# A hybrid encoder trunk with its token rows in another order: row p of tile t holds token 2p+t

## The chip, the cores and the metric

One core of one Trainium2 chip runs the whole kernel in one launch. The metric is the device time in microseconds (us); of several executions the median counts. Before the change it is 1027.39 us.

## What is computed

The trunk has two layers over 256 tokens of 1024 channels, all float32. Each layer does

```python
h = rms_norm(x, attn_pre_norm)
gates, mla_in, dil_in, diff_in = split(h @ w_in)
merged = g_mla * (mla(mla_in) @ w_branch_mla) + g_dil * (dilated(dil_in) @ w_branch_dil) \
       + g_diff * (diff(diff_in) @ w_branch_diff)
x = x + rms_norm(merged @ w_out, attn_post_norm)
h = rms_norm(x, ffn_pre_norm)
u = h @ w_up                                   # 1024 -> 2 x 2816
u = sum(shift(u, t - 1) * conv_w[t] for t in range(3))     # along the tokens
x = x + rms_norm((gelu(u_gate) * u_val) @ w_down, ffn_post_norm)
```

Two parts care about the order of the tokens. The convolution reads each token's two neighbours. The dilated attention has three groups: in the first a token sees the tokens at most 64 away, in the second those of its own class modulo 4, in the third those of its own class modulo 16 (at 256 tokens the radius excludes none of them). Everything else treats tokens alike, so long as queries, keys, values and outputs agree on which row is which token.

## The kernel before

The 256 tokens lie as two tiles of 128 rows (`x[128, 2, 1024]`). Row 64h+j of tile t holds token 4j+2t+h: each tile has two of the four classes modulo 4, one in each half of its rows. So for the second and third group of the dilated attention a tile needs only its own 128 keys. This order is set where x and the positions are loaded (lines 465, 704) and undone where the output is stored (`class_rows`, line 506).

Precision is kept by splitting: a value v becomes `hi` (a rounded copy) and `lo` = v - hi, and each product takes three matmuls, hi·lo, lo·hi and hi·hi (`passes`, line 1456). The weights pass through a ring of three buffers in 1 MB pieces, in the fixed order of `plan_pieces`. SyncE loads piece n once its buffer's `lo` has been written, ScalarE writes `w_hi` (`split_hi`, line 727), VectorE writes `w_lo` (`split_lo`, line 1083), and TensorE uses the piece. `STEPS`, one list written by `plan_steps`, is walked by TensorE, ScalarE and VectorE alike, and each does its own part of a step in that order; semaphores alone hold them together.

The MLP works the other way round. Its activations `hT` (channels on the rows, tokens on the columns) must be in true token order, since the convolution runs along the columns. `turn_ffn` (line 1722) turns x by transposes into PSUM; ScalarE's `ffn_hi` (line 839) and VectorE's `ffn_lo` (line 1110) write them to `hT_hi` and `hT_lo` through `tile_tokens` (line 536), which picks the columns of tile t: `[:, :, 2t:2t+2]` of groups of four, so two adjacent columns and then a gap of two. `scale_rows` (line 1125) does the same for the row of scales. These steps stand in "mid", between the attention sublayer and the MLP, where TensorE has nothing else but `keep_clock` transposes.

The MLP is planned in units u = 0..10: two pieces "up" (gate and value channels, 256 each; TensorE gets 128 channels by 256 tokens into PSUM), and two units later one piece "down". For each unit VectorE scales (lines 1134 to 1141), ScalarE and VectorE do the three taps of the convolution (lines 980, 1408, 1414), ScalarE the gelu (line 986), VectorE the product (`gated`, line 1148). Then ScalarE's `gated_hi` (line 858) and VectorE's `gated_lo` (line 1153) make `g_hi` and `g_lo`, and here they put the columns back in the order of the rows of x, by reading every fourth column:

```python
nc.scalar.activation(by_class2(g_hi[:, u % G_RING, :]), own_order2(conv[:, u % 2, 1, :]), ACT.Copy)
V.tensor_tensor(by_class2(g_lo[...]), own_order2(conv[...]), by_class2(g_hi[...]), ALU.subtract)
```

The piece "down" takes 128 adjacent columns of `g_hi` or `g_lo` as its stationary operand (`lhs_of`, line 1488) and 512 columns of the weights as the moving one: 2 k x 4 tiles x 3 passes = 24 matmuls a piece, 264 in a layer (the last piece of a layer takes its first tiles through `last_rows`, lines 1538 to 1544). TensorE waits for `g_lo_done` before a piece "down". In an even "up" step VectorE's order is: scale the piece, `split_lo` of a later one, `gated_lo` of the unit two before, then the convolution.

At the end of a layer ("end") ScalarE and VectorE split the first two pieces of the next layer, then do the squares (line 872), the gain (line 1256) and the residual (line 1268) of each tile, with the root from GpSimd (lines 637 to 642); TensorE turns the new x (line 1646) and goes on.

At the start GpSimd builds the mask (lines 592 to 612) while x is loaded. VectorE's `other_classes` (lines 1045 to 1052) turns row-minus-column distances, 128 columns, into the mask of the third group, then `rope_angles` follows, both in the step after piece 1; then comes `split_lo` of the pieces that TensorE needs next. GpSimd adds the result to the mask (line 653).

Of the kernel before, what the change touches and what calls it, by code (L numbers as in the profile page):

```python
# [16 lines left out]
P = 128  # L17
# [291 lines left out]
def build_trunk(nc, a, out):  # L309
    with ExitStack() as ctx:  # L310
# [111 lines left out]
        other_class = rope_b[:, 0:P]  # L422
# [42 lines left out]
        tokens = a["x"][0].rearrange("(j t h) d -> h j t d", t=NT, h=2)  # L465
# [34 lines left out]
        def own_order2(cols):  # L500
            return cols.rearrange("p (c j r) -> p c r j", c=2, r=4)

        def by_class2(cols):
            return cols.rearrange("p (c r j) -> p c r j", c=2, r=4)

        def class_rows(dram):

            view = dram[0].rearrange("(j r) d -> r j d", r=4)
            return [(slice(64 * (r % 2), 64 * (r % 2) + 64), r // 2, view[r]) for r in range(4)]
# [26 lines left out]
        def tile_tokens(cols, t):  # L536

            return cols.rearrange("p (j r) -> p j r", r=4)[:, :, 2 * t:2 * t + 2]
# [5 lines left out]
        def store_rows(eng, r_odd):  # L544

            for t in range(NT):
                for h in range(2):
                    s = slice(h * 512, h * 512 + 512)
                    part, t_of, dst = class_rows(out)[2 * t + r_odd]
                    eng.wait_ge(x_ready, X_START + 8 * DEPTH - 4 + 2 * t + h + 1)  # L550
                    eng.dma_start(dst[:, s], x[part, t_of, s]).then_inc(out_landed, 16)
# [29 lines left out]
        def _(pool):  # L581
# [13 lines left out]
            for t in range(NT):  # L595
                for h in range(2):
                    rq = 2 * t + h
                    m = mask[64 * h:64 * h + 64, t, 0:SEQ].rearrange("p (r j) -> p r j", r=4)
                    nc.gpsimd.affine_select(out=m, in_=m, compare_op=ALU.is_ge, fill=MASKED, base=rq + 64,
                                            pattern=[[-1, 4], [-4, 64]], channel_multiplier=4)  # L600
                    pool.drain()
                    nc.gpsimd.affine_select(out=m, in_=m, compare_op=ALU.is_ge, fill=MASKED, base=64 - rq,
                                            pattern=[[1, 4], [4, 64]], channel_multiplier=-4)
                    pool.drain()

            for t in range(NT):
                for g in range(2):
                    c0 = SEQ + P * g
                    nc.gpsimd.memset(mask[0:64, t, c0 + 64:c0 + 128], MASKED)
                    pool.drain()  # L610
                    nc.gpsimd.memset(mask[64:128, t, c0:c0 + 64], MASKED)
                    pool.drain()


# [29 lines left out]
            for l in range(DEPTH):  # L644
# [5 lines left out]
                if l == 0:  # L650
                    pool.wait_ge(class_ready, 1)
                    for t in range(NT):
                        nc.gpsimd.tensor_tensor(mask[:, t, 384:512], mask[:, t, 384:512], other_class, ALU.add)
# [46 lines left out]
        def _(act):  # L700
# [3 lines left out]
            positions = a["positions"][0, :].rearrange("(j t h) -> h j t", t=NT, h=2)  # L704
# [129 lines left out]
            def ffn_hi(l, t, pairs):  # L834

                for pair in pairs:
                    act.wait_ge(turn_full, l * NTURN + (TURN_BEFORE["ffn"] + FFN_FULL.index((t, pair)) + 1))
                    for k in (2 * pair, 2 * pair + 1):
                        last = nc.scalar.activation(tile_tokens(hT_hi[:, k, :], t), turned_bank(t, k).rearrange("p (h j) -> p j h", h=2), ACT.Copy,
# [12 lines left out]
            def gated_hi(l, u):  # L852
# [5 lines left out]
                nc.scalar.activation(by_class2(g_hi[:, u % G_RING, :]), own_order2(conv[:, u % 2, 1, :]), ACT.Copy).then_inc(g_hi_done, 1)  # L858
# [140 lines left out]
        def _(dve):  # L999
# [45 lines left out]
            def other_classes():  # L1045

                dve.wait_ge(distance_ready, 1)
                V.tensor_scalar(distance, distance, 3, None, ALU.bitwise_and)
                dve.drain()
                V.tensor_copy(other_class, distance)  # L1050
# [55 lines left out]
            def ffn_lo(l, t, pair):  # L1106

                dve.wait_ge(turn_hi, l * NTURN + (TURN_BEFORE["ffn"] + FFN_HI.index((t, pair)) + 1))
                for k in (2 * pair, 2 * pair + 1):
                    last = V.scalar_tensor_tensor(out=tile_tokens(hT_lo[:, k, :], t), in0=turned_bank(t, k).rearrange("p (h j) -> p j h", h=2),  # L1110
# [10 lines left out]
            def scale_rows(l):  # L1121

                dve.wait_ge(scales_full, l + 1)
                for t in range(NT):
                    V.tensor_copy(tile_tokens(token_scale, t), bank[3][:, t * P:(t + 1) * P].rearrange("p (h j) -> p j h", h=2))
# [790 lines left out]
```

## Time and profile before

| what | value |
|---|---|
| median of 3 runs | 1027.39 us (1027.29 to 1027.89) |
| the profiled execution | 1026.48 us, of which the span is 1024.7 us |
| TensorE busy | 1010.8 us |
| VectorE busy | 717.8 us |
| ScalarE busy | 589.3 us |
| GpSimd busy | 132.0 us |
| granted TensorE clock, mean | 0.998 of full speed |
| moved by DMA | 170.74 MB, 167 GB/s |

The span runs from the first to the last instruction; the time adds what lies around it, 1.8 us here. In the rows below, PE is TensorE's matmul, PEld its weight load, DVE VectorE, ACT ScalarE, POOL GpSimd. PE's durations are modelled and overlap: it is the distance from one start to the next that counts, not the sum.

### The profile page before, as it was taken

What the parts mean: (1) busy time and instruction counts of PE and PEld (TensorE: products, weight loads), DVE (VectorE), ACT (ScalarE), POOL (GpSimd) and SP (SyncE); (2) the same over time, 40 slices, a digit from 0 to 9 for tenths busy, and PEclk for the clock granted to TensorE, in tenths of its full rate; (3) what the DMA queues carried; (4) which work ended last, traced back from release to release, by engine and by line L of the source; (5) the groups of instructions that cost most, each with busy time, mean ns of one, the idle gap of its engine ahead of it and who ended that gap; (6) DMA issues with size and microseconds to landing.
All of it is one profiled execution on the core that took longest, in us unless ns stands there. A gap on an engine that the chain in (4) does not pass through costs nothing.

```text
span 1024.7 us, 15035 instructions
## 1 busy us (share of the span) xinstructions
PE 1010.8 (99%) x5764; PEld 883.3 (86%) x5764; DVE 717.8 (70%) x962; ACT 589.3 (58%) x859; POOL 132.0 (13%) x257
## 2 busy tenths in 40 slices
PE   8999999999999999999999999999999999999997
PEld 8889999888888988888888899998888889888886
DVE  5635566555586899999875355666555869899996
ACT  5657666565446555555575666665663556555553
POOL 3353124000001000000024321230000020000000
PEclk9999999999999999999999999999999999999999
DMA  8555445454445565555364544465335644655541
GB/s 254 184 169 161 123 132 178 165 165 164 144 135 174 186 226 174 196 190 180 123 200 160 169 131 123 143 217 164 124 127 181 203 145 166 213 198 186 184 164 42
DMA packets 109035, 170.74 MB, mean 167 GB/s; under 512 B 3377, under 2 KB 72804, under 8 KB 108964
## 3 DMA queue, kind: packets, MB, share of 16 engines
q1 hardware_dynamic: 107676, 166.88, 50.1%
q10 hardware_dynamic: 1208, 2.63, 0.8%
q8 instruction: 46, 0.75, 0.3%
q0 software_dynamic: 80, 0.26, 0.1%
q14 instruction: 25, 0.20, 0.1%
HBM read 168.72 MB, written 1.05 MB: 166 GB/s over the span
## 4 chain that ended last, share of the span: by engine, by line
PE 94%; DVE 2%; ACT 1%; DVEq 1%; issue 1%; POOL 0%; POOLq 0%; ACTq 0%
PE bank L1458 20%; PE bank L1460 19%; PE bank L1459 19%; PE high_banks L1468 10%; PE high_banks L1466 5%; PE high_banks L1864 2%; PE high_banks L1458 2%; PE high_banks L1459 2%; PE high_banks L1460 2%; PE high_banks L1465 1%; PE high_banks L1765 1%; PE high_banks L1786 1%; PE high_banks L1857 1%; PE high_banks L1774 1%; PE high_banks L1802 1%
## 5 line engine op out<-in xcount | busy, mean ns | idle before, releaser
L1083 DVE TENSOR_TENSOR w_lo<-w_raw,w_hi 128x2048 fp32r<-128x2048 f32 (+3 forms) x174 | 364.1, 2095 | 160.1 <-ACT w_hi L727 159.8
L727 ACT ACTIVATE w_hi<-w_raw 128x2048 fp32r<-128x2048 f32 (+3 forms) x174 | 305.0, 1754 | 139.0 <-PE high_banks L1468 92.5
L1458 PE MATMUL bank<-w_hi,hT 128*128 128x512 f32 (+2 forms) x700 | 258.5, 369 | 1.5 <-DVE hT L1162 0.7
L1460 PE MATMUL bank<-w_hi,hT 128*128 128x512 f32 (+2 forms) x700 | 252.9, 361 | 0.0
L1459 PE MATMUL bank<-w_lo,hT 128*128 128x512 f32 (+2 forms) x700 | 252.5, 361 | 0.0
L1468 PE MATMUL high_banks<-hT,w_hi 128*128 128x512 f32 x420 | 149.8, 396 | 0.0
L1458 PEld LDWEIGHTS bank<-w_hi,hT 128*128 128x128 f32 x700 | 131.5, 188 | 17.6 <-issue 2.9
L1460 PEld LDWEIGHTS bank<-w_hi,hT 128*128 128x128 f32 x700 | 131.4, 188 | 14.1
L1459 PEld LDWEIGHTS bank<-w_lo,hT 128*128 128x128 f32 x700 | 131.7, 188 | 13.0
L1466 PE MATMUL high_banks<-hT,w_lo 128*128 128x256 f32 x480 | 124.0, 279 | 0.0
L1466 PEld LDWEIGHTS high_banks<-hT,w_lo 128*128 128x128 f32 x480 | 90.5, 188 | 5.2
L1468 PEld LDWEIGHTS high_banks<-hT,w_hi 128*128 128x128 f32 x420 | 78.8, 188 | 16.3
L637 POOL TENSOR_SCALAR mean_squares<-small 128x1 f32<-128x1 f32 x12 | 7.6, 633 | 596.1 <-ACT x_normed L872 580.4
L980 ACT ACTIVATE conv_out<-up_scaled,par_all 128x256 f32<-128x256 f32 x88 | 40.0, 502 | 49.9 <-DVE up_scaled L1141 22.2
L1458 PE MATMUL bank<-w_hi,g_lo 128*128 128x512 f32 x168 | 66.6, 396 | 0.0
L1459 PE MATMUL bank<-w_lo,g_hi 128*128 128x512 f32 x168 | 65.5, 390 | 0.0
L1460 PE MATMUL bank<-w_hi,g_hi 128*128 128x512 f32 x168 | 65.5, 390 | 0.0
L1458 PE MATMUL high_banks<-hT,w_lo 128*128 128x256 f32 x208 | 59.2, 284 | 0.7 <-DVE hT L1110 0.7
L1459 PE MATMUL high_banks<-hT,w_hi 128*128 128x256 f32 x208 | 58.8, 283 | 0.0
L1460 PE MATMUL high_banks<-hT,w_hi 128*128 128x256 f32 x208 | 58.8, 283 | 0.0
L626 POOL TENSOR_TENSOR rope_a<-stage,cosT 128x96 f32<-128x96 f32 (+1 forms) x40 | 28.9, 723 | 164.4 <-ACT stage L746 136.2
L1139 DVE TENSOR_REDUCE up_scaled<-high_banks 128x512 f32<-128x1024 f32 x30 | 36.6, 1221 | 12.3 <-PE high_banks L1468 12.3
(244 smaller groups left out, 1508.2 us busy)
## 6 DMA issues: line engine op xcount, KB each, us to landing
w_raw<-in_w_up_dram SPq DMA_DIRECT2D x44, 1024.0 KB, 5.0
w_raw<-in_w_in_dram SPq DMA_DIRECT2D x36, 1024.0 KB, 5.0
w_raw<-in_w_in_dram SPq DMA_DIRECT2D x36, 768.0 KB, 4.3
w_raw<-in_w_down_dram SPq DMA_DIRECT2D x22, 1024.0 KB, 4.8
w_raw<-in_w_out_dram SPq DMA_DIRECT2D x8, 1024.0 KB, 5.0
w_raw<-in_w_in_dram SPq DMA_DIRECT2D x8, 672.0 KB, 4.1
w_raw<-in_w_branch_mla_dram SPq DMA_DIRECT2D x4, 1024.0 KB, 4.9
w_raw<-in_w_branch_diff_dram SPq DMA_DIRECT2D x4, 1024.0 KB, 4.9
```

The source lines that it names most:

```text
L626: nc.gpsimd.tensor_tensor(ca, xr, c, ALU.mult)
L727: nc.scalar.activation(w_hi[:, n % RING, 0:nk * cols], raw[:, n % RING, 0:nk * cols], ACT.Copy).then_inc(hi_done, 1)
L980: last = nc.scalar.activation(conv[:, u % 2, b, j * SEQ:(j + 1) * SEQ], up_scaled[:, c % 2, j, :], ACT.Copy, scale=par_all[:, l, 44 + ch:4 ...
L1083: V.tensor_tensor(w_lo[:, n % RING, s], raw[:, n % RING, s], w_hi[:, n % RING, s].bitcast(F32), ALU.subtract).then_inc(lo_done, 1)
L1139: V.tensor_reduce(up_scaled[:, c % 2, :, :], up_banks(c).rearrange("p j (s q) -> p j q s", s=2), AX.X, ALU.add).then_inc(up_summed, 1)
L1458: PE.matmul(dst, lhs[1], rhs_hi, start=start, stop=False)
L1459: PE.matmul(dst, lhs[0], rhs_lo, start=False, stop=False)
L1460: return PE.matmul(dst, lhs[0], rhs_hi, start=False, stop=stop)
L1465: PE.matmul(dst, w_parts[0], hT[:, k, :, :], start=True, stop=False)
L1466: last = PE.matmul(dst[:, 0:SEQ], w_parts[1], hT_hi[:, k, :], start=False, stop=False)
L1468: last = PE.matmul(dst, w_parts[0], hT[:, k, :, :], start=False, stop=k == KD - 1)
L1864: last = PE.transpose(T_BANK[:, b * P:(b + 1) * P], probs[:, i % 2, b * P:(b + 1) * P], ident[:])
```

## The change

The rows of x now hold token 2p+t in row p of tile t. Then a tile's tokens are every second column of the token order. The products of the MLP stay in token order, so `gated_hi` and `gated_lo` read and write adjacent columns, and the piece "down" takes every second column of `g_hi` and `g_lo` as its stationary operand. `tile_tokens` becomes every second column too, for `hT_hi`, `hT_lo` and the scales, read from adjacent columns of PSUM. A tile still holds whole classes modulo 4 (rows of one parity each), so the second and third group need their own 128 keys as before, but both masks are now made from distances, by `& 1` and `& 7`: the eight fills of half tiles go, eight half-height selections become four of full height, and VectorE's `other_classes` has one more instruction and 256 columns in place of 128 in two others. GpSimd adds 256 columns to the mask in place of 128.

```diff
-        other_class = rope_b[:, 0:P]
+        distance_8 = rope_a[:, P:2 * P].bitcast(I32)
+        distances = rope_a[:, 0:2 * P].bitcast(I32)
+        other_class = rope_b[:, 0:2 * P]
...
-        tokens = a["x"][0].rearrange("(j t h) d -> h j t d", t=NT, h=2)
+        tokens = a["x"][0].rearrange("(h j t) d -> h j t d", h=2, t=NT)
...
-        def class_rows(dram):
-            view = dram[0].rearrange("(j r) d -> r j d", r=4)
-            return [(slice(64 * (r % 2), 64 * (r % 2) + 64), r // 2, view[r]) for r in range(4)]
+        def rows_of(dram):
+            view = dram[0].rearrange("(h j t) d -> h t j d", h=2, t=NT)
+            return [(slice(64 * h, 64 * h + 64), t, view[h, t]) for t in range(NT) for h in range(2)]
...
         def tile_tokens(cols, t):
-            return cols.rearrange("p (j r) -> p j r", r=4)[:, :, 2 * t:2 * t + 2]
+            return cols.rearrange("p (m r) -> p m r", r=NT)[:, :, t]
...
             for t in range(NT):
-                for h in range(2):
-                    rq = 2 * t + h
-                    m = mask[64 * h:64 * h + 64, t, 0:SEQ].rearrange("p (r j) -> p r j", r=4)
...
-            for t in range(NT):
-                for g in range(2):
-                    c0 = SEQ + P * g
-                    nc.gpsimd.memset(mask[0:64, t, c0 + 64:c0 + 128], MASKED)
-                    nc.gpsimd.memset(mask[64:128, t, c0:c0 + 64], MASKED)
+                m = mask[:, t, 0:SEQ].rearrange("p (r j) -> p r j", r=NT)
+                nc.gpsimd.affine_select(out=m, in_=m, compare_op=ALU.is_ge, fill=MASKED, base=t + 64,
+                                        pattern=[[-1, NT], [-2, P]], channel_multiplier=2)
+                nc.gpsimd.affine_select(out=m, in_=m, compare_op=ALU.is_ge, fill=MASKED, base=64 - t,
+                                        pattern=[[1, NT], [2, P]], channel_multiplier=-2)
...
-                        nc.gpsimd.tensor_tensor(mask[:, t, 384:512], mask[:, t, 384:512], other_class, ALU.add)
+                        nc.gpsimd.tensor_tensor(mask[:, t, 256:512], mask[:, t, 256:512], other_class, ALU.add)
...
-            positions = a["positions"][0, :].rearrange("(j t h) -> h j t", t=NT, h=2)
+            positions = a["positions"][0, :].rearrange("(h j t) -> h j t", h=2, t=NT)
...
-                        last = nc.scalar.activation(tile_tokens(hT_hi[:, k, :], t), turned_bank(t, k).rearrange("p (h j) -> p j h", h=2), ACT.Copy,
+                        last = nc.scalar.activation(tile_tokens(hT_hi[:, k, :], t), turned_bank(t, k), ACT.Copy,
...
-                nc.scalar.activation(by_class2(g_hi[:, u % G_RING, :]), own_order2(conv[:, u % 2, 1, :]), ACT.Copy).then_inc(g_hi_done, 1)
+                nc.scalar.activation(g_hi[:, u % G_RING, :], conv[:, u % 2, 1, :], ACT.Copy).then_inc(g_hi_done, 1)
...
-                V.tensor_scalar(distance, distance, 3, None, ALU.bitwise_and)
+                V.tensor_scalar(distance_8, distance, 7, None, ALU.bitwise_and)
                 dve.drain()
-                V.tensor_copy(other_class, distance)
+                V.tensor_scalar(distance, distance, 1, None, ALU.bitwise_and)
+                dve.drain()
+                V.tensor_copy(other_class, distances)
...
-                    last = V.scalar_tensor_tensor(out=tile_tokens(hT_lo[:, k, :], t), in0=turned_bank(t, k).rearrange("p (h j) -> p j h", h=2),
+                    last = V.scalar_tensor_tensor(out=tile_tokens(hT_lo[:, k, :], t), in0=turned_bank(t, k),
...
-                    V.tensor_copy(tile_tokens(token_scale, t), bank[3][:, t * P:(t + 1) * P].rearrange("p (h j) -> p j h", h=2))
+                    V.tensor_copy(tile_tokens(token_scale, t), bank[3][:, t * P:(t + 1) * P])
...
-                V.tensor_tensor(by_class2(g_lo[:, u % G_RING, :]), own_order2(conv[:, u % 2, 1, :]),
-                                by_class2(g_hi[:, u % G_RING, :].bitcast(F32)), ALU.subtract).then_inc(g_lo_done, 1)
+                V.tensor_tensor(g_lo[:, u % G_RING, :], conv[:, u % 2, 1, :],
+                                g_hi[:, u % G_RING, :].bitcast(F32), ALU.subtract).then_inc(g_lo_done, 1)
...
-                return g_hi[:, u % G_RING, k * SEQ + t * P:k * SEQ + t * P + P], g_lo[:, u % G_RING, k * SEQ + t * P:k * SEQ + t * P + P]
+                own = slice(k * SEQ, (k + 1) * SEQ)
+                return tile_tokens(g_hi[:, u % G_RING, own], t), tile_tokens(g_lo[:, u % G_RING, own], t)
```

## Rows read from the trace of the kernel before

**Rows 1.** The page: busy time by engine, and the chain that ended last.

```profile
PE 1010.8 (99%) x5764; PEld 883.3 (86%) x5764; DVE 717.8 (70%) x962; ACT 589.3 (58%) x859; POOL 132.0 (13%) x257
PE 94%; DVE 2%; ACT 1%; DVEq 1%; issue 1%; POOL 0%; POOLq 0%; ACTq 0%
```

**Rows 2.** The page's costliest groups: busy us, mean ns, idle before and releaser.

```profile
L858 ACT ACTIVATE g_hi<-conv_out 128x512 fp32r<-128x512 f32 x22 | 24.9, 1133 | 9.8 <-DVE conv_out L1148 9.8
L1153 DVE TENSOR_TENSOR g_lo<-conv_out,g_hi 128x512 fp32r<-128x512 f32 x22 | 23.6, 1073 | 3.5 <-ACT g_hi L858 3.5
L1148 DVE TENSOR_TENSOR conv_out<-conv_out 128x512 f32<-128x512 f32 x22 | 15.1, 684 | 0.2
L986 ACT ACTIVATE conv_out<-conv_out 128x512 f32<-128x512 f32 x22 | 13.6, 619 | 0.0
```

**Rows 3.** Timeline (start us, us) where a "down" piece begins, the first held one.

```profile
379.81 0.40 PE L1468 MATMUL high_banks<-hT,w_hi 128*128 128x512 f32 x1
380.08 0.47 PE L1458 MATMUL bank<-w_hi,g_lo 128*128 128x512 f32 x1
380.38 0.39 PE L1459 MATMUL bank<-w_lo,g_hi 128*128 128x512 f32 x1
380.61 0.40 PE L1460 MATMUL bank<-w_hi,g_hi 128*128 128x512 f32 x1
...
380.05 0.19 PEld L1458 LDWEIGHTS bank<-w_hi,g_lo 128*128 128x128 f32 x1 [0.16 <-issue]
...
378.87 1.06 DVE L1153 TENSOR_TENSOR g_lo<-conv_out,g_hi 128x512 fp32r<-128x512 f32 x1
```

**Rows 4.** Timeline at the last held "down" piece of the second layer.

```profile
984.38 0.47 PE L1458 MATMUL bank<-w_hi,g_lo 128*128 128x512 f32 x1
```

**Rows 5.** Timeline of VectorE and TensorE at the start.

```profile
20.84 0.22 DVE L1048 TENSOR_SCALAR rope_a<-rope_a 128x128 int32<-128x128 int32 x1
21.13 0.23 DVE L1050 CAST rope_b<-rope_a 128x128 f32<-128x128 int32 x1
...
27.86 0.50 PE L1458 MATMUL bank<-w_hi,hT 128*128 128x512 f32 x1 [0.60 <-DVE w_lo L1083]
```

**Rows 6.** Timeline between the layers, then the same steps at the kernel's end.

```profile
510.89 0.60 ACT L872 ACTIVATE x_normed<-bank 128x512 f32<-128x512 f32 x1 [0.31 <-PE bank L1544]
...
509.41 3.03 DVE L1083 TENSOR_TENSOR w_lo<-w_raw,w_hi 128x1344 fp32r<-128x1344 f32 x2
513.98 1.41 DVE L1268 SCALAR_TENSOR_TENSOR x_rows<-square_ffn,roots,x_rows 128x512 f32<-128x512 f32 x2
...
1014.64 0.60 ACT L872 ACTIVATE x_normed<-bank 128x512 f32<-128x512 f32 x1 [2.76 <-PE bank L1544]
...
1017.01 1.41 DVE L1268 SCALAR_TENSOR_TENSOR x_rows<-square_ffn,roots,x_rows 128x512 f32<-128x512 f32 x2 [0.29 <-POOL roots L642]
```

**Rows 7.** Lines 839, 848, 1110, 1162: duration ns as min/median/max, first and last start.

```profile
L839 ACT ACTIVATE hT<-bank,par_all x20: 364/383/423, 324.4 to 832.4; 128x128 fp32r<-128x128 f32 x20
...
L848 ACT ACTIVATE hT<-bank,par_all x4: 360/369/382, 520.1 to 520.9; 128x128 fp32r<-128x128 f32 x4
...
L1110 DVE SCALAR_TENSOR_TENSOR hT<-bank,par_all,hT x20: 339/342/352, 326.9 to 834.7; 128x128 fp32r<-128x128 f32 x20
...
L1162 DVE SCALAR_TENSOR_TENSOR hT<-bank,par_all,hT x4: 343/345/351, 520.8 to 521.6; 128x128 fp32r<-128x128 f32 x4
```

**Rows 8.** Timeline in the first "mid" step: VectorE, and TensorE's first two pieces "up".

```profile
331.39 2.28 DVE L1083 TENSOR_TENSOR w_lo<-w_raw,w_hi 128x2048 fp32r<-128x2048 f32 x1
...
328.33 0.36 PE L1458 MATMUL high_banks<-hT,w_lo 128*128 128x256 f32 x1 [0.33 <-DVE hT L1110]
...
334.15 0.28 PE L1458 MATMUL high_banks<-hT,w_lo 128*128 128x256 f32 x1
```

**Rows 9.** Timeline of GpSimd in the second layer: rotary product for diff, then for uq.

```profile
542.49 0.46 POOL L627 TENSOR_TENSOR rope_b<-stage,sinT 128x128 f32<-128x128 f32 x1
...
554.63 0.45 POOL L627 TENSOR_TENSOR rope_b<-stage,sinT 128x128 f32<-128x128 f32 x1
```

More of the change, by code:

```diff
@@ L498, in by_class @@
             return cols.rearrange("p (r j) -> p r j", r=4)
[L500 to L504, printed above, removed]
-        def class_rows(dram):
-            view = dram[0].rearrange("(j r) d -> r j d", r=4)
-            return [(slice(64 * (r % 2), 64 * (r % 2) + 64), r // 2, view[r]) for r in range(4)]
+        def rows_of(dram):
+            view = dram[0].rearrange("(h j t) d -> h t j d", h=2, t=NT)
+            return [(slice(64 * h, 64 * h + 64), t, view[h, t]) for t in range(NT) for h in range(2)]
         def wait_tile(eng, l, m):
@@ L548, in store_rows @@
                     s = slice(h * 512, h * 512 + 512)
-                    part, t_of, dst = class_rows(out)[2 * t + r_odd]
+                    part, t_of, dst = rows_of(out)[2 * t + r_odd]
                     eng.wait_ge(x_ready, X_START + 8 * DEPTH - 4 + 2 * t + h + 1)
@@ L595, in _ @@
             for t in range(NT):
-                for h in range(2):
-                    rq = 2 * t + h
-                    m = mask[64 * h:64 * h + 64, t, 0:SEQ].rearrange("p (r j) -> p r j", r=4)
[L599 to L604, printed above, removed]
-            for t in range(NT):
-                for g in range(2):
-                    c0 = SEQ + P * g
-                    nc.gpsimd.memset(mask[0:64, t, c0 + 64:c0 + 128], MASKED)
-                    pool.drain()
-                    nc.gpsimd.memset(mask[64:128, t, c0:c0 + 64], MASKED)
-                    pool.drain()
+                m = mask[:, t, 0:SEQ].rearrange("p (r j) -> p r j", r=NT)
+                nc.gpsimd.affine_select(out=m, in_=m, compare_op=ALU.is_ge, fill=MASKED, base=t + 64,
+                                        pattern=[[-1, NT], [-2, P]], channel_multiplier=2)
+                pool.drain()
+                nc.gpsimd.affine_select(out=m, in_=m, compare_op=ALU.is_ge, fill=MASKED, base=64 - t,
+                                        pattern=[[1, NT], [2, P]], channel_multiplier=-2)
+                pool.drain()
             def rope(view, heads, first, half, t):
```

## The prediction, made before the change was run

> **What bounds the kernel now.** I read the page first: TensorE is busy for 99% of the span and 94% of the chain that ended last is matmuls [rows 1]. So a microsecond is gained only where a matmul starts late, and lost only where one starts later than now. VectorE and ScalarE have idle time on the whole. Next I went through the timeline for places where the distance between two matmul starts is above its usual one. Usual is 0.23 us after a matmul of 512 columns, as from 380.38 to 380.61 [rows 3]. The change touches four places that stand out.
>
> First, the start of a piece "down". The last matmul of the piece "up" starts at 379.81 and VectorE's g_lo ends at 378.87 + 1.06 = 379.93. Only at 380.05 does the first weight load begin, 0.16 us after TensorE could have had it, and the first matmul shows 0.47 us where others show 0.39: 0.31 us to the next start [rows 3]. From 379.81 to 380.38 it is 0.57 us where two usual distances make 0.46, so 0.11 us are lost. The wait is on g_lo, not on "issue", as the row puts it: the load starts 0.12 us after g_lo ends, every time. There are 7 such starts in each layer, 14 in all, from 380.08 to 984.38 [rows 3, 4]; the other 8 of the 22 show no 0.47.
>
> Second, the start of the kernel: at 27.86 TensorE has waited 0.60 us for w_lo, which stands on VectorE behind `other_classes` and the angles [rows 5]. Third, the step from layer to layer, where VectorE is behind. Fourth, "mid", where TensorE waits for hT [rows 8].
>
> **The change part by part.**
>
> *g_hi and g_lo (adjacent columns).* Today these are the only 512-column operations that read every fourth column: 1133 ns against 619 ns for a plain one on ScalarE, 1073 against 684 on VectorE [rows 2]. Both fall to the plain values: minus 0.51 us on ScalarE and minus 0.39 us on VectorE, 22 times each. That is 20 us of engine time, and nearly all of it lies beside matmuls. What counts is that g_lo ends 0.39 us earlier, at about 379.54, before 379.81, when the weight load could go. The wait disappears: 14 x 0.11 = **-1.5 us**. Nothing else is late there: w_lo of that piece is done before g_lo starts (378.87), since one engine makes both. If something else holds it, the term is 0; it can't be more than 14 x 0.13 = 1.8.
>
> *Between the layers.* ScalarE's squares start at 510.89, the residual at 513.98: 3.09 us. At the kernel's end the same steps take 1014.64 to 1017.01: 2.37 us [rows 6]. The difference, 0.72 us, is there because VectorE is still splitting two pieces until 509.41 + 3.03 = 512.44. This split comes after g_lo and g_hi of the last two units, which lie one behind the other in that stretch, and ScalarE's w_hi follows its second g_hi: 0.51 + 0.39 + 0.51 = 1.4 us less stand ahead of that w_hi and so of the split, which is over at about 511.0, before the first squares are done at 511.5. I take the whole **-0.7 us**; the bounds are -0.3 (GpSimd's root stays where it is) and -0.72.
>
> *The masks.* GpSimd's work in the first ten microseconds shrinks, and nobody waits for it before the dilated attention: 0. VectorE has one more instruction, 0.29 us from start to start (20.84 to 21.13), a CAST and a comparison of 256 columns in place of 128. The wide ones cost 128 columns more each; at most (0.684 - 0.23) / 384 = 1.2 ns a column [rows 2, 5], 0.15 us each, at least nothing. I take 0.1 each. All of it stands ahead of the w_lo for which TensorE waits at 27.86, so it comes out whole: **+0.5 us**, between 0.3 and 0.6. After that TensorE doesn't wait, so nothing gives it back.
>
> *hT and the scales, every second column.* Today's pattern is two adjacent columns and a gap of two, and it costs nothing on VectorE (342 against 345 ns for the plain line 1162) and 14 ns on ScalarE (383 against 369) [rows 7]. No row shows a write of every second column. Lower bound: 14 ns gained each, two of them on the path in each layer, nothing to speak of. Upper bound: the rate at which every fourth column costs today, (1133 - 619) / 512 = 1.0 ns a column on ScalarE and (1073 - 684) / 512 = 0.76 on VectorE. The nearest row to a step of two is GpSimd's: for "diff" it reads sinT in steps of two, for "uq" in steps of one, and takes 0.46 and 0.45 us [rows 9]. I take 0 by that row.
>
> *The weights of "down", every second column.* No row shows it either. By the same argument: 0, and upper bound 1.0 ns a column. What that would cost is less than it seems. The load at 380.05 lets its matmul flow 0.08 us later than the start shown (0.47 against 0.39), that is about 0.11 us after the load's start, and the next load begins with the current matmul [rows 3]. So a load may take 0.23 us before a matmul of 512 columns is held up.
>
> *Loads and stores of x, positions.* As many bytes and rows as before, other addresses: 0, give or take 0.2.
>
> Here a rule and a rule differ. Rows first: every fourth column costs, pairs cost nothing [rows 2, 7]. The Trainium skill's page "SBUF — State Buffer", section "Specifications (TRN2)", says that full bandwidth needs at least two accesses to each 16-byte line; float32 in steps of two has two, in steps of four one. Its page "Vector Engine (DVE) Microarchitecture Reference", section "Measured stream behaviour on trn2", says that a port is at full rate only with runs of two adjacent words, and loses some 0.65 cycle an element otherwise. Both fit every row here; they part at a step of two, and the second speaks against the change. It makes the second rival below.
>
> Sum: -1.5 - 0.7 + 0.5 = **-1.7 us**. The profiled execution took 1026.48 us, so 1024.8; it stands 0.9 below the median of the runs, and against that median, 1027.39, the forecast is **1025.7 us**.
>
> **The rivals.**
>
> *A: the wait moves.* The piece "down" is held as before by something that g_lo now hides. For it: g_lo would end only 0.27 us before 379.81, and 0.12 of that goes until the load can start. Against: VectorE takes up its slack only once in a cycle and nothing else in it changed. Price: the 1.5 us stay. 1027.2 us.
>
> *B: writing and reading every second column costs on ScalarE and VectorE.* Place: "mid", twice. Two operations on ScalarE and two on VectorE before TensorE's first matmul at 328.33: 2 x 0.13 + 2 x 0.10 = 0.45 us. Then w_lo of the second piece, which ends at 331.39 + 2.28 = 333.67 for a start at 334.15 [rows 8], comes 16 x 0.097 = 1.55 us later, at 335.2: 1.1 us late in all, more if in1 and out both pay. So 2.3 us for both layers, up to 5. 1028.0 us. For: the rate at a step of four. Against: the GpSimd rows. The second page named above gives this case.
>
> *C, the slower side: the strided weight load outlasts its matmul.* Place: the 528 stationary operands of "down". It decides from 0.227 us a load: at 0.11 now, plus 128 x 1.0 ns by ScalarE's rate, it is 0.24, so 12 ns too long, 528 x 0.012 = 6.3 us. At VectorE's rate, 0.11 + 0.10 = 0.21, it would be hidden completely. 1025.7 + 6.3 = 1032.0 us, 0.4% slower. Against: the same rows as against B, and that load must be hit harder than doubled.
>
> **How the numbers follow.** Forecast 0.65, A 0.10, B 0.13, C 0.12. What a measurement of this kernel can tell from no change is about 0.2%, 2.05 us. The forecast lies 1.7 below, with terms open by some 0.7 both ways, so it counts 0.28 faster and the rest same; A and most of B are same; C and the top of B slower: 0.28, 0.56, 0.16. The range runs from 1024.4 (all terms at their good ends, 0.4 for the addresses of x) to 1029.2, which holds A and most of B and leaves C out.
>
> **What would show it.** Right: g_hi at 0.62 and g_lo at 0.68 us; no first matmul of "down" with 0.47, and the cycle of two pieces "up" and one "down" 0.1 us shorter; lines 839 and 1110 at today's durations; TensorE waiting about 1.1 us in place of 0.6 before its first 512-column piece; residual 2.4 us after the squares between the layers. Wrong: matmuls of "down" more than 0.23 apart, lines 839 and 1110 at 0.45 us or more, or a second "up" piece that waits for w_lo.

## The result, and the profile after

The changed kernel takes 1028.84 us in the median against 1026.62 us for the kernel before, 22 executions each. The medians are 2.2 us apart; the ratio that compares the two kernels is 1.0017, with a 95% interval from 1.0011 to 1.0023: slower by 1.8 us, where 1.7 us less was forecast. The time lies inside the range, the sign is wrong. One execution of the changed kernel took 2033.79 us; it isn't in that ratio, and nothing recorded says why it was slow. The 1027.39 us from which the forecast started was the median of three executions. The profiled execution of the changed kernel took 1028.2 us, with a span of 1026.4 us; the span before was 1024.7, so the two traces hold 1.7 us of the difference.

The page of the changed kernel, busy time and the chain, against [rows 1]:

```profile
PE 1011.5 (99%) x5764; PEld 885.6 (86%) x5764; DVE 710.6 (69%) x963; ACT 579.3 (56%) x859; POOL 127.4 (12%) x245
...
PE 95%; DVE 1%; ACT 1%; DMA 1%; issue 1%; DVEq 0%; SPq 0%; POOL 0%; POOLq 0%
```

VectorE, ScalarE and GpSimd all have less to do, 22 us in all. TensorE has as many instructions and is busy 0.7 us more; its weight loads take 2.3 us more. That is where to look: the engine that bounds got slower at work whose count didn't change.

The groups of g_hi and g_lo and of the weight loads (PEld), shapes apart: busy us, mean ns, idle before and releaser. The first two answer to [rows 2].

```profile
L842 ACT ACTIVATE g_hi<-conv_out 128x512 fp32r<-128x512 f32 x22 | 13.6, 618 | 8.7 <-DVE conv_out L1134 8.7
L1139 DVE TENSOR_TENSOR g_lo<-conv_out,g_hi 128x512 fp32r<-128x512 f32 x22 | 15.1, 686 | 1.9 <-ACT g_hi L842 1.9
...
L1444 PEld LDWEIGHTS bank<-w_hi,g_lo 128*128 128x128 f32 x168 | 32.4, 193 | 6.0
L1444 PEld LDWEIGHTS bank<-w_hi,hT 128*128 128x128 f32 x700 | 131.5, 188 | 18.7 <-issue 3.0 <-DVE w_lo L1069 2.2 <-DVE hT L1087 0.2
```

g_hi and g_lo fell to 618 and 686 ns, as forecast. The loads of `g_lo` now take 193 ns, those of `hT`, which this change leaves adjacent, 188. In the kernel before both took 188.

The timeline where the first piece "down" begins that was held before (start us, us), against [rows 3]:

```profile
380.18 0.69 DVE L1139 TENSOR_TENSOR g_lo<-conv_out,g_hi 128x512 fp32r<-128x512 f32 x1
...
381.13 0.39 PE L1454 MATMUL high_banks<-hT,w_hi 128*128 128x512 f32 x1
381.13 0.19 PEld L1444 LDWEIGHTS bank<-w_hi,g_lo 128*128 128x128 f32 x1
381.36 0.39 PE L1444 MATMUL bank<-w_hi,g_lo 128*128 128x512 f32 x1
...
381.59 0.39 PE L1445 MATMUL bank<-w_lo,g_hi 128*128 128x512 f32 x1
...
381.83 0.39 PE L1446 MATMUL bank<-w_hi,g_hi 128*128 128x512 f32 x1
...
382.06 0.39 PE L1444 MATMUL bank<-w_hi,g_lo 128*128 128x512 f32 x1
```

The wait is gone: g_lo ends at 380.87, and the weight load goes at 381.13 with the last matmul of "up". But the matmuls of "down" now start 0.23 to 0.24 us apart. Over the whole trace the median distance after one of them is 233 ns, against 227 before. Six nanoseconds don't show in one row; they show in the pace of the cycle of two pieces "up" and one "down". From the first to the seventh of the held starts it took 16.762 us before (380.077 to 480.649) and takes 16.787 now (381.360 to 482.080), though each cycle lost a wait.

The timelines of the start: GpSimd, VectorE and TensorE (start us, us, idle before), against [rows 5]:

```profile
22.50 1.31 POOL L637 TENSOR_TENSOR mask<-mask,rope_b 128x256 bf16<-128x256 bf16 x2 [4.21 <-DVE rope_b L1038]
...
21.15 0.22 DVE L1032 TENSOR_SCALAR rope_a<-rope_a 128x128 int32<-128x128 int32 x1
21.45 0.23 DVE L1034 TENSOR_SCALAR rope_a<-rope_a 128x128 int32<-128x128 int32 x1
21.75 0.30 DVE L1036 CAST rope_b<-rope_a 128x256 f32<-128x256 int32 x1
22.13 0.29 DVE L1038 TENSOR_SCALAR rope_b<-rope_b 128x256 f32<-128x256 f32 x1
22.34 0.16 DVE L1003 CAST pos_f<-pos_i 128x2 f32<-128x2 int32 x1
22.57 0.65 DVE L1006 TENSOR_TENSOR ang<-pos_f,inv_freq 128x32 f32<-128x32 f32 x1
23.30 0.55 DVE L1010 TENSOR_SCALAR turns<-ang 128x32 f32<-128x32 f32 x1
...
29.11 0.50 PE L1444 MATMUL bank<-w_hi,hT 128*128 128x512 f32 x1 [1.53 <-DVE w_lo L1069]
```

TensorE's first matmul of 512 columns went from 27.86 to 29.11, by 1.25 us. Three causes lie in it. `other_classes` takes 1.19 us (21.15 to 22.34) in place of 0.73: the 0.46 that was forecast. The next two instructions, on 32 columns each, take 0.65 and 0.55 us; before they took 0.41 and 0.30. That is 0.49 more, and it wasn't forecast. They run while GpSimd adds to the mask, 1.31 us in two parts in place of 0.82. The rows show how. The second addition ends at 22.50 + 1.31 = 23.81 and the instruction beside it at 23.30 + 0.55 = 23.85. In the kernel before, the additions end at 22.17 and 22.56 and the two instructions at 22.22 and 22.60. Each time VectorE's instruction is over 0.04 to 0.05 us after GpSimd's, as if it had waited for it. The remaining 0.3 us were there before this stretch began: the first matmul on weights started at 11.54 in place of 11.22.

Between the layers, VectorE and ScalarE, against [rows 6]:

```profile
511.82 1.56 DVE L1069 TENSOR_TENSOR w_lo<-w_raw,w_hi 128x1344 fp32r<-128x1344 f32 x1 [0.99 <-ACT w_hi L711]
...
515.10 1.42 DVE L1254 SCALAR_TENSOR_TENSOR x_rows<-square_ffn,roots,x_rows 128x512 f32<-128x512 f32 x2 [0.28 <-POOL roots L626]
...
510.46 1.33 ACT L711 ACTIVATE w_hi<-w_raw 128x1344 fp32r<-128x1344 f32 x1 [1.22 <-PE bank L1446]
512.73 0.60 ACT L856 ACTIVATE x_normed<-bank 128x512 f32<-128x512 f32 x1 [0.95 <-PE bank L1531]
```

From the first squares to the residual it is 2.37 us, where it was 3.09; before, only the steps at the kernel's end took 2.37. And the writes to every second column of `hT`, by line (duration ns as min/median/max), against [rows 7]:

```profile
L823 ACT ACTIVATE hT<-bank,par_all x20: 364/382/421, 325.6 to 833.5; 128x128 fp32r<-128x128 f32 x20
...
L1096 DVE SCALAR_TENSOR_TENSOR hT<-bank,par_all,hT x20: 341/345/352, 328.1 to 835.8; 128x128 fp32r<-128x128 f32 x20
```

They cost what they did: 382 against 383 ns, 345 against 342.

### The profile page after: what moved, and what is told of

Its sections match the earlier page's. It is cut to its first block, busy times and chain, and to the rows that moved or that the text cites. A ratio compares the mean times of both kernels' runs of the same rounds, so it can differ in the third digit from the quotient of the medians.

```text
span 1026.4 us, 15009 instructions
## 1 busy us (share of the span) xinstructions
PE 1011.5 (99%) x5764; PEld 885.6 (86%) x5764; DVE 710.6 (69%) x963; ACT 579.3 (56%) x859; POOL 127.4 (12%) x245
## 4 chain that ended last, share of the span: by engine, by line
PE 95%; DVE 1%; ACT 1%; DMA 1%; issue 1%; DVEq 0%; SPq 0%; POOL 0%; POOLq 0%
PE bank L1444 20%; PE bank L1446 20%; PE bank L1445 20%; PE high_banks L1454 10%; PE high_banks L1452 5%; PE high_banks L1444 2%; PE high_banks L1445 2%; PE high_banks L1446 2%; PE high_banks L1851 2%; PE high_banks L1451 1%; PE high_banks L1752 1%; PE high_banks L1773 1%; PE high_banks L1844 1%; PE high_banks L1761 1%; PE high_banks L1789 1%; PE high_banks L1796 1%
```

## The experiments

The first theory: a stationary operand of every second column costs 6 ns in each of the 528 matmuls of "down", 3.2 us, and that outweighs the gain at g_hi and g_lo. The rival: the loss is at the start, or in something that comes with the new order.

**One part alone: adjacent g_hi and g_lo.** The kernel before with only these two operations changed. The products of "down" then meet the columns in another order.

```diff
-                nc.scalar.activation(by_class2(g_hi[:, u % G_RING, :]), own_order2(conv[:, u % 2, 1, :]), ACT.Copy)...
+                nc.scalar.activation(g_hi[:, u % G_RING, :], conv[:, u % 2, 1, :], ACT.Copy)...
...
-                V.tensor_tensor(by_class2(g_lo[:, u % G_RING, :]), own_order2(conv[:, u % 2, 1, :]),
-                                by_class2(g_hi[:, u % G_RING, :].bitcast(F32)), ALU.subtract)...
+                V.tensor_tensor(g_lo[:, u % G_RING, :], conv[:, u % 2, 1, :],
+                                g_hi[:, u % G_RING, :].bitcast(F32), ALU.subtract)...
```

> The kernel before, in which g_hi and g_lo alone copy adjacent columns (the product then meets the columns in another order than the rows of x: the output is not the reference's). Theory: g_hi falls from 1.13 to 0.62 us and g_lo from 1.07 to 0.69, the 14 held starts of a piece down vanish (-1.5 us) and the step between the layers gets 0.77 us shorter: -2.3 us in all, the matmuls of down stay 227 ns apart. Rival (the gain of the changed kernel came with its new row order, not with the plain copies): no change.

Measured: 1024.1 us, ratio 0.9971 (0.9959 to 0.9983); span 1022.1, 2.6 less than before. The cycle of two pieces "up" and one "down" is 16.627 us, 0.135 shorter than before, and its "down" matmuls stay 227 ns apart. So the gain that the prediction counted on is there, all of it, and a little more.

**One part alone: the stepped weights of "down".** The kernel before with only `lhs_of` changed; it too multiplies the columns in another order.

```diff
-                return g_hi[:, u % G_RING, k * SEQ + t * P:k * SEQ + t * P + P], g_lo[...]
+                own = slice(k * SEQ, (k + 1) * SEQ)
+                every = lambda g: g[:, u % G_RING, own].rearrange("p (m r) -> p m r", r=2)[:, :, t]
+                return every(g_hi), every(g_lo)
```

> The kernel before, in which the pieces down take every second column of g_hi and g_lo as stationary operand and nothing else is changed (wrong columns, so the output is not the reference's). Theory: the step of two alone makes the start-to-start distance of these matmuls 233 ns in place of 227, 528 x 6 ns = +3.0 to +3.2 us. Rival (the 6 ns come from the unheld rhythm of the pieces, as the 233 ns that other matmuls show in both kernels): distance 227, 0 us.

Measured: 1029.34 us, ratio 1.0023 (1.0014 to 1.0032); span 1027.4, 2.7 more. Its loads and matmuls, from the timeline:

```profile
380.51 0.39 PE L1459 MATMUL bank<-w_lo,g_hi 128*128 128x512 f32 x1
380.75 0.39 PE L1460 MATMUL bank<-w_hi,g_hi 128*128 128x512 f32 x1
380.98 0.39 PE L1458 MATMUL bank<-w_hi,g_lo 128*128 128x512 f32 x1
381.21 0.39 PE L1459 MATMUL bank<-w_lo,g_hi 128*128 128x512 f32 x1
381.44 0.39 PE L1460 MATMUL bank<-w_hi,g_hi 128*128 128x512 f32 x1
```

Four distances make 0.93 us, 233 ns each. It is 2.7 us in the span and not 3.2, since here the 14 starts are still held, and 64 more of the 527 distances that the trace of the kernel before has, some behind each held start, were already 231 ns or more. With both parts changed the step costs the full amount: from the kernel with adjacent g to the changed one the two MLP stretches grow by about 1.65 us each. The step takes back all that the adjacent g gives, 2.6 us, and some more.

**Twice the step.** The same with every fourth column, for rival C. The 128 columns of a product come from both halves of the unit.

```diff
-                return g_hi[:, u % G_RING, k * SEQ + t * P:k * SEQ + t * P + P], g_lo[...]
+                every = lambda g: g[:, u % G_RING, :].rearrange("p (m r) -> p m r", r=4)[:, :, 2 * k + t]
+                return every(g_hi), every(g_lo)
```

> The kernel before with every fourth column of g_hi and g_lo as stationary operand of down (wrong columns, the output is not the reference's). Theory 1, a longer load that peeks out from under a matmul of 512 columns: a step of four is slower still, load near 0.24 to 0.30 us, distance 240 to 300 ns, +7 to +40 us. Theory 2, a fixed cost of any stepped pattern: distance 233 again, +3 us.

Measured: 1031.85 us, ratio 1.0046 (1.0032 to 1.006); span 1030.0. Timeline of the loads, then of the matmuls, at a held start:

```profile
380.22 0.31 PEld L1458 LDWEIGHTS bank<-w_hi,g_lo 128*128 128x128 f32 x1 [0.16 <-issue]
...
380.70 0.31 PEld L1460 LDWEIGHTS bank<-w_hi,g_hi 128*128 128x128 f32 x1
380.93 0.31 PEld L1458 LDWEIGHTS bank<-w_hi,g_lo 128*128 128x128 f32 x1
...
380.25 0.60 PE L1458 MATMUL bank<-w_hi,g_lo 128*128 128x512 f32 x1
380.69 0.40 PE L1459 MATMUL bank<-w_lo,g_hi 128*128 128x512 f32 x1
380.93 0.40 PE L1460 MATMUL bank<-w_hi,g_hi 128*128 128x512 f32 x1
```

The span is 5.3 us longer: above theory 2, below the range of theory 1. A load takes 310 ns now, 122 more than an adjacent one, and the matmuls are 0.24 us apart all the same; the median distance is 237 ns, and in a row they alternate between 231 and 238 to 240. 122 / 128 is 0.95 ns a column, close to the 1.0 that ScalarE pays for every fourth one; at a step of two the same sum is 5 / 128 = 0.04. So the load is hardly longer at a step of two, and even at four it lies almost wholly beside a matmul of 512 columns. In these rows one load, 380.70 to 381.01, isn't over when the next begins at 380.93. So the prediction's limit, 0.23 us a load before a matmul is held up, doesn't hold for the length that a row shows, and rival C's mechanism was priced too high. What costs is 6 ns a matmul that the length of the load doesn't explain.

**The same step in another stage: "up".** The kernel before with the stationary operand of the pieces "up", which is the weights there, taken by every second column; channels mix.

```diff
-                        w_parts = (hi[:, k, j * P:(j + 1) * P], lo[:, k, j * P:(j + 1) * P])
+                        w_parts = tuple(x[:, k, :].rearrange("p (m r) -> p m r", r=2)[:, :, j] for x in (hi, lo))
```

> The kernel before, in which the stationary operands of the pieces up (weights) are every second column, under matmuls of 256 columns with little room to hide a load (wrong channels, the output is not the reference's). Theory 1, the load takes about twice as long and is hidden under 512 columns but for 6 ns: the matmuls of 256 columns in the first six pieces go from 120 ns apart to about 200, +50 us and more in all. Theory 2, a fixed small cost: 120 to about 126 ns, and 1168 + 960 such matmuls make about +8 to +12 us.

One execution: 1026.76 us, span 1025.0, 0.3 more than before; loads 195 to 196 ns in place of 188 to 192, and no median distance changed. A matmul of 256 columns is followed after 120 ns, and the pairs of 512 and 256 go at 233 and 117 ns, as before. Neither theory's number came.

**And in "gate" and "dil".** The kernel before with `hT` stepped in the products of the gates (576 matmuls of 512 columns) and of the dilated branch (864 of 384); rows of both tiles mix.

```diff
+                if kind in ("dil", "gate"):
+                    return tuple(v[:, k, :].rearrange("p (m r) -> p m r", r=2)[:, :, t] for v in (hT_hi, hT_lo))
```

> The kernel before with every second column of hT as stationary operand in the pieces gate (576 matmuls of 512 columns) and dil (864 of 384 columns), wrong tokens, so the output is not the reference's. Theory 1 (a step of two costs every matmul that sets the pace itself 6 ns): 227 to 233 ns and 173 to 179 ns, +8.6 us. Theory 2 (it is particular to g_hi and g_lo, their place or the piece down): no change. Between them (only at 512 columns): +3.5 us.

Measured: 1030.52 us, ratio 1.004 (1.0024 to 1.0055); span 1028.2, 3.5 more. The median distance in "gate" went from 227 to 233 and 235 ns; 576 x 6 ns is 3.5 us, the whole difference. In "dil" it stayed at 173. Of seven starts in a row in "gate" the first and the last, six distances of 233 ns:

```profile
186.64 0.39 PE L1459 MATMUL bank<-w_lo,hT 128*128 128x512 f32 x1
...
188.04 0.39 PE L1459 MATMUL bank<-w_lo,hT 128*128 128x512 f32 x1
```

So the price isn't one of the piece "down" but of a stepped stationary operand where one matmul of 512 columns follows another; at 384 and at 256 columns, and in the pairs of 512 and 256 of the pieces "up", the same step is free.

**The changed kernel without the step.** All of the change, but g_hi and g_lo read every second column and write each tile's 128 side by side, so that "down" takes adjacent ones. Nothing is left out.

```diff
-                nc.scalar.activation(g_hi[:, u % G_RING, :], conv[:, u % 2, 1, :], ACT.Copy)...
+                nc.scalar.activation(g_hi[:, u % G_RING, :].rearrange("p (c t m) -> p c t m", c=2, t=NT),
+                                     conv[:, u % 2, 1, :].rearrange("p (c m t) -> p c t m", c=2, t=NT), ACT.Copy)...
...
-                return tile_tokens(g_hi[:, u % G_RING, own], t), tile_tokens(g_lo[:, u % G_RING, own], t)
+                return g_hi[:, u % G_RING, k * SEQ + t * P:k * SEQ + t * P + P], g_lo[...]
```

> The changed kernel, in which g_hi and g_lo read every second column and write a tile's columns side by side, so that down takes adjacent columns again; it computes the same. Theory (the stepped stationary operand costs 6 ns a matmul, while ScalarE and VectorE read steps of two at full rate): distance 233 to 227 ns, 528 x 6 ns = -3.2 us, g_hi stays at 0.62 and g_lo at 0.69 us, no held start. Rival (a step of two costs ScalarE and VectorE part of what a step of four did): g_lo at 0.85 us or more, the held starts come back for some 1.5 us, -1.7 us.

Measured: 1025.18 us, ratio to the kernel before 0.9988 (0.9979 to 0.9997); span 1023.1, 3.3 below the changed kernel. Its two groups:

```profile
L842 ACT ACTIVATE g_hi<-conv_out 128x512 fp32r<-128x512 f32 x22 | 14.6, 662 | 8.7 <-DVE conv_out L1135 8.7
...
L1140 DVE TENSOR_TENSOR g_lo<-conv_out,g_hi 128x512 fp32r<-128x512 f32 x22 | 15.1, 687 | 2.0 <-ACT g_hi L842 2.0
```

Reading every second column costs VectorE 1 ns in 686 and ScalarE 44 in 618. The distance in "down" is 227 ns again. Of the 3.3 us, 3.2 lie in the two MLP stretches, and 0.3 in an earlier first matmul on weights; small changes elsewhere go the other way. So the step's 3.2 us are shown from both sides, by putting it in and by taking it out.

**The masks alone.** The kernel before with the mask code of the changed one: GpSimd's selections, `other_classes` and the wider addition. The mask doesn't fit the order of the rows then.

```diff
-                V.tensor_scalar(distance, distance, 3, None, ALU.bitwise_and)
+                V.tensor_scalar(distance_8, distance, 7, None, ALU.bitwise_and)
+                dve.drain()
+                V.tensor_scalar(distance, distance, 1, None, ALU.bitwise_and)
...
-                        nc.gpsimd.tensor_tensor(mask[:, t, 384:512], mask[:, t, 384:512], other_class, ALU.add)
+                        nc.gpsimd.tensor_tensor(mask[:, t, 256:512], mask[:, t, 256:512], other_class, ALU.add)
```

> The kernel before with the mask code of the changed one alone (the masks then don't fit the rows, so the output is not the reference's). Theory: other_classes 0.46 us longer, the two next operations of the angles 0.48 us slower beside GpSimd's wider addition, so TensorE's first matmul of 512 columns at 28.8 in place of 27.9 us, +0.9 us. Rival (the slower angles come from where the code lies, not from GpSimd): +0.5 us.

Measured: 1027.5 us, ratio 1.0011 (1.0001 to 1.002). From the first matmul on weights to the first of 512 columns it is 17.55 us, against 16.64 before and 17.57 in the changed kernel: 0.91 us for the masks, nearly twice the 0.5 forecast.

**GpSimd's addition made narrow again.** The changed kernel, but GpSimd adds only the last 128 columns; the second group goes without its mask.

```diff
-                        nc.gpsimd.tensor_tensor(mask[:, t, 256:512], mask[:, t, 256:512], other_class, ALU.add)
+                        nc.gpsimd.tensor_tensor(mask[:, t, 384:512], mask[:, t, 384:512], other_class[:, P:2 * P], ALU.add)
```

> The changed kernel, in which GpSimd adds only the 128 columns of the third group to the mask (the second group goes unmasked, so the output is not the reference's). Theory (GpSimd's wider addition slows the angles by 0.48 us): the first matmul of 512 columns 17.1 us after the first on weights in place of 17.6. Rival (where the instructions lie in memory): 17.6 still.

One execution, for the start alone (1028.88 us, span 1027.1). Its VectorE and GpSimd there:

```profile
23.60 0.40 DVE L1006 TENSOR_TENSOR ang<-pos_f,inv_freq 128x32 f32<-128x32 f32 x1
24.08 0.30 DVE L1010 TENSOR_SCALAR turns<-ang 128x32 f32<-128x32 f32 x1
...
23.52 0.82 POOL L637 TENSOR_TENSOR mask<-mask,rope_b 128x128 bf16<-128x128 bf16 x2 [4.19 <-DVE rope_b L1038]
```

The two instructions are back at 0.40 and 0.30 us, and the same stretch is 17.07 us, 0.50 less. So an addition that is 0.49 us shorter takes as much off VectorE: that GpSimd's addition delays the instructions beside it is shown.

The span didn't follow, because the first matmul on weights came at 12.57, 1.0 us later than in the changed kernel. TensorE's transposes of x, in the changed kernel and then here, with its granted clock from 9.3 to 12.5 us (0.50, the number before the last two of the row):

```profile
8.47 1.94 PE L1687 MATMUL high_banks<-ident,x_rows 128*128 128x128 f32 x16 [1.24 <-issue]
...
9.27 3.56 PE L1687 MATMUL high_banks<-ident,x_rows 128*128 128x128 f32 x16 [2.29 <-issue]
...
9.30:12.50 3.20, 3.20 (x16) 3.20 (x16) 0.88 (x2) 2.04 (x4) 0.00 (x0) 0.50 0.97 351
```

The first transpose began 0.8 us later, TensorE had stood idle 2.29 us before it in place of 1.24, and the 16 transposes then ran at the lower of its two clock levels, 213 ns apart in place of 109. The same happened in the profile of the next experiment (9.24 us, 2.12 us idle, 213 ns), and in no other of the fourteen.

**`other_classes` early.** The changed kernel, but VectorE does it ahead of its first step, at 5 us, where it has nothing to do.

```diff
+            other_classes()
             for l in range(DEPTH):
...
                     elif what == "angles" and l == 0:
-                        other_classes()
```

> The changed kernel, in which VectorE works out other_classes at about 5 us, where it waits for hT, and not between the pieces; it computes the same. Theory (1.19 us of other_classes and 0.48 us by which GpSimd's wider addition slows the angles stand on TensorE's way to its first matmul of 512 columns): that start comes 1.6 us earlier, at about 27.5 in place of 29.1 us, -1.6 us. Rival (only the added 0.46 us count, the rest is hidden by the loads of the weights): -0.5 us.

Measured: 1027.74 us, ratio 1.0007 (0.9998 to 1.0017). The span of the profile, 1026.3, shows little of the gain, since x came late there. The stretch from the first matmul on weights to the first of 512 columns shrank from 17.57 to 16.53 us, by 1.04 and not by the 1.6 expected. The reason stands in the timelines of GpSimd and VectorE:

```profile
19.04 4.00 POOL L637 TENSOR_TENSOR mask<-mask,rope_b 128x256 bf16<-128x256 bf16 x2
...
19.00 3.51 DVE L1069 TENSOR_TENSOR w_lo<-w_raw,w_hi 128x1344 fp32r<-128x1344 f32 x2 [1.05 <-ACT w_hi L711]
22.43 0.64 DVE L1003 CAST pos_f<-pos_i 128x2 f32<-128x2 int32 x1
```

GpSimd still adds in its own place, behind a root, and no longer waits for VectorE there, so the addition fell beside w_lo. It took 4.00 us in place of 1.31, w_lo 3.51 in place of 3.03, and the CAST behind it 0.64 in place of 0.16. These rows too look like taking turns: the first addition ends at 21.09, 0.53 us after the first w_lo (20.56), the second w_lo then lasts until 22.51, the second addition ends 0.53 us after that, at 23.04, and the CAST at 23.07.

**Both mends.** `other_classes` early and "down" without the step.

> The changed kernel with both edits, adjacent columns for down and other_classes early; it computes the same. If the two costs are independent: -3.2 - 1.6 = -4.8 us against the changed kernel, about 3 us below the kernel before. If the second is hidden: -3.7 us.

Measured: 1024.64 us, ratio 0.998 (0.9971 to 0.9989); span 1022.1. That is 4.3 us below the changed kernel, between the two numbers expected: 3.3 from the step and 1.0 from `other_classes`. So the two costs add up, the second with what it gave alone in the stretch at the start.

**And GpSimd's addition early too.** The last kernel, with the addition moved ahead of GpSimd's first root, so that it runs at 6.72, right behind `other_classes`. Nothing is left out.

```diff
+            pool.wait_ge(class_ready, 1)
+            for t in range(NT):
+                nc.gpsimd.tensor_tensor(mask[:, t, 256:512], mask[:, t, 256:512], other_class, ALU.add)
+            pool.drain().then_inc(masks_ready, 1)
             for l in range(DEPTH):
```

> The kernel with both edits (adjacent columns for down, other_classes early) and GpSimd's addition to the mask early too, at about 7 us while VectorE is idle; it computes the same. Theory (GpSimd's addition and VectorE slow each other whenever they meet: in the kernel with other_classes early it took 4.0 us beside w_lo and made w_lo 0.5 and the cast of the positions 0.5 us longer): the first matmul of 512 columns comes another 0.65 us earlier, that is all that TensorE still waits there, about 15.9 us after the first matmul on weights in place of 16.5. Rival (w_lo is slow there for another reason): no change.

Measured: 1023.75 us, ratio 0.997 (0.9958 to 0.9981). This version beats both kernels: the one before by 3.1 us, the changed one by about 5 (from the two ratios). The addition takes 1.30 us at 6.72. The stretch is 15.86 us, against 16.53 in the last one. VectorE's w_lo ends 0.97 us earlier in it, but only 0.67 reach TensorE, for now it has no wait left at that place:

```profile
27.31 0.32 PE L1447 MATMUL bank<-w_lo,hT 128*128 128x336 f32 x1
27.47 0.32 PE L1448 MATMUL bank<-w_hi,hT 128*128 128x336 f32 x1
27.62 0.39 PE L1446 MATMUL bank<-w_hi,hT 128*128 128x512 f32 x1
```

The first matmul of 512 columns follows the last of 336 after 0.15 us, with no idle time. The 0.60 us of [rows 5] are gone, and w_lo, over at 24.98 + 2.29 = 27.27, is no longer what the start hangs on.

**The new order of x alone.** The kernel before with only the rows of x taken in the new order.

```diff
-        tokens = a["x"][0].rearrange("(j t h) d -> h j t d", t=NT, h=2)
+        tokens = a["x"][0].rearrange("(h j t) d -> h j t d", h=2, t=NT)
```

> The kernel before, in which x alone is loaded in the new order (the tokens are then mixed up, so the output is not the reference's). Theory (the later start of the changed kernel's first matmul on weights, 11.54 against 11.22 us, is scatter of the landings): 11.2 to 11.3 us as in four other profiles with the old order. Rival (rows 8 KB apart load slower than rows 16 KB apart): 11.5 us.

One execution: 1027.27 us, span 1025.5. The first matmul on weights starts at 12.04, and the stretch behind it is 16.66 us, as before. In the seven traces with the old order of x that first matmul comes between 11.17 and 11.48 us, in the seven with the new one between 11.24 and 12.57, in the mean 11.27 and 11.83. Two of the seven with the new order have the halved clock described above. What stands ahead of that is clearer: TensorE's first transpose of x starts at 8.01 to 8.34 us with the old order (mean 8.18) and at 8.33 to 9.27 with the new one (mean 8.77; 8.92 here). The two sets touch at one value only. The time that the packets of x took doesn't tell them apart: summed over the 256 of them it is 63.0 us before, 71.8 in the changed kernel, 61.8 here. So the traces point to half a microsecond for the new order at the start, more than the prediction's 0.2, but only one execution has that order and nothing else, and what delays x stays open.

## Why the prediction was wrong

- **Held starts of "down": -1.5 us. Right, and slightly short.** All 14 waits are gone. With adjacent columns in "down" the cycle is 0.135 us shorter; the span of that kernel is 2.6 less, 0.7 of it between the layers, so 1.9 here. That is 0.1 above the upper bound given. The two distances that the prediction counted at each start give 1.5, as forecast; the rest comes from the ones behind them, which had been a few nanoseconds long too.
- **Between the layers: -0.7. Right,** 3.09 us became 2.37, but with less to spare than argued. The split was over 1.55 us after the first squares began and is now over 0.65 after: 0.9 us gained and not 1.4, since ScalarE's second w_hi waits for TensorE. GpSimd helped: its first instruction for the root took 0.84 us beside w_lo and takes 0.22 behind it.
- **The weights of "down", every second column: 0. This is the step that failed.** It measured 6 ns x 528 = 3.2 us. The argument bounded the load, found that up to 0.23 us of it is hidden, and took hidden for free. The load did stay hidden: 193 ns, 5 more. But the distance of the matmuls grew by 6 ns with it. A difference of 6 ns was far below anything that the prediction asked about, and 528 times it is twice the forecast gain. The bound was drawn in nanoseconds a column; it should have been drawn a second time in nanoseconds a matmul: 1 ns on each of the 528 is 0.5 us. The range held the time by luck: rivals B and A had stretched it upwards, and neither of them is what happened.
- **The masks: +0.5, at most 0.6. The term was mis-sized:** 0.9 us. The three counted instructions took 0.46, as forecast. GpSimd's wider addition has no term in the sum. The prediction looked at who waits for GpSimd, found nobody, and not at who runs beside it; the addition costs VectorE 0.49 more, ahead of the w_lo that TensorE waits for.
- **hT and the scales: 0. Right,** and rival B falls with it. No second "up" piece waits for w_lo more than before.
- **Rival A** fell: nothing took the place of the wait. **Rival C** had the place right, and the sign, but not the mechanism: no load outlasts its matmul.
- **Loads of x: 0, give or take 0.2.** The first matmul on weights came 0.3 later in the profiled execution; whether the order of x is the cause is only pointed to.
- The sum with the measured terms: -1.9 - 0.7 + 3.2 + 0.9 + 0.3 is +1.8 us, against +1.7 in the span and +1.8 from the ratio.

On the two pages weighed: the Trainium skill, "SBUF — State Buffer", section "Specifications (TRN2)", asks for two accesses to a 16-byte line. The traces agree for VectorE (345 ns written at a step of two, 687 read) and for the load's length, 193 ns at two and 310 at four; ScalarE's read at two costs 44 ns in 618, less than a tenth of the 514 that four costs. "Vector Engine (DVE) Microarchitecture Reference" of the Trainium skill, section "Measured stream behaviour on trn2", asks for runs of two adjacent words. The traces disagree at a step of two: 687 against 686 ns.

What stays open is why 512 columns pay the 6 ns. The pieces "up" show 233 ns after a matmul of 512 columns with adjacent columns already, where the next has 256, and don't pay again when stepped. I have no run that tells what the 6 ns are.

## What to carry over

Where the engine that bounds repeats an instruction hundreds of times, an "almost hidden" change to its operand must be priced per instruction, in single nanoseconds, and not by whether it fits under its neighbour; reorder in the copies that another engine makes anyway, where here it cost 44 ns 22 times beside other work. Work that nobody waits for still has a price when it runs beside the engine that somebody waits for. Moving it is only worth as much as the place that it moves to: put it where both are idle.

## What the runs showed that I had not expected

- A stationary operand of every second column: load 193 in place of 188 ns, and the next start after 233 in place of 227 ns where 512 columns follow 512 (528 and 576 matmuls, three kernels); nothing at 384 (173 ns), at 256 (120 ns) or in pairs of 512 and 256 (233 and 117 ns). Of every fourth: load 310 ns, next start 237.
- GpSimd and VectorE delay each other: an addition of 256 bf16 columns, twice, took GpSimd 1.31 us beside small VectorE instructions and 4.00 beside w_lo, which itself lost 0.48 us; two VectorE instructions of 32 columns took 0.65 and 0.55 us beside it, 0.40 and 0.30 beside the narrower addition, and 0.19 and 0.18 alone. The instruction of the one ends just behind that of the other, so what counts is how long the other's instruction is.
- In the two profiles in which x came latest (9.24 and 9.27 us), TensorE stood idle for over 2 us before it, and the 16 transposes then took 3.4 to 3.6 us at a granted clock of about half, in place of 1.9.
